# One core: four query projections and half of the output layer moved between the attention's steps, probabilities scaled on ScalarE

## The chip, the cores and the metric

The kernel runs on one core of a Trainium2 chip. The metric is the device time of one execution in microseconds (us). The engines are called by their short names: PE (TensorE, matrix multiply; PEld is its weight load), DVE (VectorE), ACT (ScalarE), POOL (GpSimd) and SP (SyncE, which issues the weight DMAs). They run their own instruction streams in order and wait for one another on semaphores.

## What is computed

One inference step of a two-layer decoder on T = 288 tokens: 256 of a prompt and 8 x 4 of eight samples. Layer 0 is a convolution module and a dense SwiGLU. Then keys and values are projected, and layer 1 is a sliding-window attention with a sink and a mixture of 8 experts. The change lies in the attention of layer 1:

```python
hq = rms_norm(h, P['g_attn_norm'][j])
q = rms_norm((hq @ P['w_q'][j]).reshape(N, T, N_KV_HEADS, GROUP, HEAD_DIM), P['g_q_norm'][j])
...
s = jnp.einsum('bnqkgd,bnskd->bnkgqs', qb, kb).astype(jnp.float32) * (HEAD_DIM ** -0.5)
s = s + rel_bias_heads(rel_bias, dist)
s = jnp.where(valid[None, :, None, None], s, -jnp.inf)
...
m = jnp.maximum(jnp.max(s, axis=-1, keepdims=True), sink)
p = jnp.exp(s - m)
denom = jnp.sum(p, axis=-1, keepdims=True) + jnp.exp(sink - m)
return jnp.einsum(eq, (p / denom).astype(v.dtype), v)
...
h = h + o @ P['w_o'][j]
```

There are 16 query heads of 64 channels in 4 groups, one key head for each group, and blocks of 128 positions; a query block sees itself and the block before.

## The kernel before

**Precision and weights.** Large products are made from three matmuls in fp32r (`mm3`, L352): high part by high part, high by low, low by high. Each weight unit of 128 x 2048 comes by DMA into one of six `land` buffers, ACT casts it into `w_hi` (`hi_to`), and DVE subtracts to make `w_lo` (`lo_to`), in a ring of four. PE frees a slot with `used`.

**Query projection** (L530 to L547). Eight tiles of 128 channels (two heads of two groups each), each 24 matmuls of 288 columns. ACT copies a tile to `Q`, POOL multiplies it by the token's inverse norm, ACT squares it, PE takes the mean over a head (`head_mean`), ACT takes the root, DVE makes the reciprocal and multiplies (`head_norm`, L1364).

**Attention** (L549 to L642). Nine steps in the order of `STEPS`: (n, b) is head group n with query block b (b = 0 has one key block, b = 1 two), and `None` is all samples. In a step PE makes the scores (`scores`), DVE adds the bias and finds the maximum (`soft_args`), ACT takes the exponentials (`exps`), DVE multiplies by the inverse sum (`normalise`, L1427), PE transposes the probabilities (`turn_probs`), ACT copies them out of PSUM (`pT`), and PE multiplies by the values (`attend`). After the second group of a pair ACT and DVE split the result into `H_hi` and `H_lo` (`o_hi`, `o_lo`).

**The order of the work** is written out by hand, on each engine for itself. At step s, PE issues scores(s+2), attend(s-1), turn_probs(s); DVE issues soft_args(s+1), normalise(s), o_lo(s-1); ACT issues exps(s+1), o_hi(s-1), and the pT copies of s. Between two steps PE has no other work, except five matmuls on constants ahead of the first transposes (`FILL`, L588).

**Output layer** (L674 to L687). Eight tiles of 24 matmuls with `w_o`; after each, the sums of two tiles earlier for the router (`route_sums`, `to_tokens`). Then the routing, the gathering of rows and the loop over experts, which is two thirds of the time.

## Time and profile before

| what | value |
|---|---|
| median of 3 runs | 1561.8 us (1558.99 to 1562.72) |
| the profiled execution | 1560.62 us |
| its span | 1558.8 us |
| mean granted TensorE clock | 0.986 of full speed |
| PE busy | 1520.7 us, 98% of the span, 7891 instructions |
| DVE, ACT, POOL busy | 1218.9, 969.2, 116.4 us |
| chain that ended last | PE 92%, DVE 3%, DMA 2%, ACT 1% |

The profiled execution is one run; its time is the span and some 2 us around it. Busy PE time is modelled at the ends of matmuls, which are pipelined, so that two matmuls that overlap both count. A granted clock of 1.00 is 2.4 GHz and 0.50 is 1.2 GHz. Times in a view count from the start of the span. An idle time in brackets stands before the instruction, with the one that released it.

### The profile page before, as it was taken

To read this page: it belongs to the slowest core of one execution; us is meant where nothing else is said; L and a number is where in the kernel's file an instruction comes from. 1 tells how busy PE (TensorE), PEld (TensorE's weight loads), DVE (VectorE), ACT (ScalarE), POOL (GpSimd) and SP (SyncE) were. 2 spreads that over 40 slices of the span, in tenths; PEclk is the share of its full clock that TensorE was granted. 3 is DMA by queue.
4 is the path that set the end of the run, shared out by engine and by line. 5 is a ranking of instruction groups with operands and counts; after the bars stand their busy time and mean duration, and the time that the engine had idled before them with its cause. 6 is when DMAs were issued, how large, how long until landed. Compare 5 with 4: busy or idle time off the path is not lost.

```text
span 1558.8 us, 22061 instructions
## 1 busy us (share of the span) xinstructions
PE 1520.7 (98%) x7891; PEld 1284.1 (82%) x7891; DVE 1218.9 (78%) x1237; ACT 969.2 (62%) x1072; POOL 116.4 (7%) x99
## 2 busy tenths in 40 slices
PE   8998999999989989999999999999999999999998
PEld 6986999999975968888888888888888888888776
DVE  6995545446696458888888889889889889889886
ACT  6554443344564247677777677777777677767764
POOL 1001011011320010000000000000000000000000
PEclk9999999999998979999999999999999999999999
DMA  8930345444531549989989998998998998998992
GB/s 348 175 128 27 108 162 177 144 156 150 187 123 50 193 177 372 367 310 404 398 321 385 395 356 349 401 381 321 412 373 314 422 370 309 423 377 300 414 366 106
DMA packets 66259, 438.48 MB, mean 281 GB/s; under 512 B 8069, under 2 KB 10373, under 8 KB 15648
## 3 DMA queue, kind: packets, MB, share of 16 engines
q1 hardware_dynamic: 57312, 412.38, 67.6%
q0 software_dynamic: 5552, 19.36, 5.1%
q10 hardware_dynamic: 3344, 6.05, 1.1%
q8 instruction: 33, 0.54, 0.1%
q14 instruction: 18, 0.15, 0.0%
HBM read 423.73 MB, written 15.03 MB: 281 GB/s over the span
## 4 chain that ended last, share of the span: by engine, by line
PE 92%; DVE 3%; DMA 2%; ACT 1%; issue 1%; POOL 1%; SPq 0%; ACTq 0%; DVEq 0%; POOLq 0%
PE bank L354 27%; PE bank L356 27%; PE bank L355 27%; PE bank L402 3%; PE bank L779 2%; DMA land<-in_w_expert 1%; PE bank L376 1%; DMA land<-in_w_dense 1%; PE bank L628 0%; PE bank L711 0%; PE bank L602 0%; PE bank L657 0%; PE bank L717 0%; PE bank L580 0%; PE bank L617 0%
## 5 line engine op out<-in xcount | busy, mean ns | idle before, releaser
L1474 DVE TENSOR_TENSOR w_lo<-land,w_hi 128x2048 fp32r<-128x2048 f32 x224 | 504.3, 2289 | 78.2 <-ACT w_hi L1078 76.3
L1078 ACT CAST w_hi<-land 128x2048 fp32r<-128x2048 f32 x224 | 418.5, 1913 | 6.4 <-issue 3.5
L354 PE MATMUL bank<-w_hi,xe_hi 128*128 128x512 f32 x896 | 364.8, 407 | 1.6 <-DVE xe_lo L1560 1.0
L356 PE MATMUL bank<-w_hi,xe_lo 128*128 128x512 f32 x896 | 354.3, 395 | 0.0
L355 PE MATMUL bank<-w_lo,xe_hi 128*128 128x512 f32 x896 | 353.0, 394 | 0.0
L1573 DVE TENSOR_TENSOR d_lo<-land,d_hi 128x2048 fp32r<-128x2048 f32 x112 | 256.8, 2292 | 44.6 <-ACT d_hi L1081 43.7
L1081 ACT CAST d_hi<-land 128x2048 fp32r<-128x2048 f32 x112 | 213.9, 1911 | 122.3 <-PE bank L356 119.1
L356 PEld LDWEIGHTS bank<-w_hi,xe_lo 128*128 128x128 f32 x896 | 168.4, 188 | 39.4
L354 PEld LDWEIGHTS bank<-w_hi,xe_hi 128*128 128x128 f32 x896 | 169.0, 189 | 36.2 <-DVE xe_lo L1560 1.2
L355 PEld LDWEIGHTS bank<-w_lo,xe_hi 128*128 128x128 f32 x896 | 169.1, 189 | 34.1
L354 PE MATMUL bank<-d_hi,heT_hi 128*128 128x512 f32 x448 | 177.3, 396 | 1.1 <-DVE heT_lo L1605 1.1
L355 PE MATMUL bank<-d_lo,heT_hi 128*128 128x512 f32 x448 | 177.1, 395 | 0.0
L356 PE MATMUL bank<-d_hi,heT_lo 128*128 128x512 f32 x448 | 176.3, 394 | 0.0
L1196 DVE TENSOR_TENSOR w_lo<-land,w_hi 128x2048 fp32r<-128x2048 f32 (+1 forms) x56 | 128.2, 2295 | 26.5 <-ACT w_hi L845 26.3
L354 PE MATMUL bank<-G_hi,w_hi 128*128 128x288 f32 x416 | 124.7, 300 | 0.3 <-PE bank L356 0.3
L355 PE MATMUL bank<-G_lo,w_hi 128*128 128x288 f32 x416 | 122.7, 295 | 0.0
L356 PE MATMUL bank<-G_hi,w_lo 128*128 128x288 f32 x416 | 122.3, 294 | 0.0
L845 ACT CAST w_hi<-land 128x2048 fp32r<-128x2048 f32 (+1 forms) x56 | 104.4, 1871 | 24.5 <-PE bank L356 22.2
L1153 ACT CAST heT_hi<-bank 128x256 fp32r<-128x256 f32 x112 | 41.8, 373 | 123.2 <-PE bank L779 123.2
L354 PEld LDWEIGHTS bank<-d_hi,heT_hi 128*128 128x128 f32 x448 | 84.2, 188 | 22.3 <-issue 2.5
L356 PEld LDWEIGHTS bank<-d_hi,heT_lo 128*128 128x128 f32 x448 | 84.5, 189 | 20.1
L355 PEld LDWEIGHTS bank<-d_lo,heT_hi 128*128 128x128 f32 x448 | 84.5, 189 | 19.0
(264 smaller groups left out, 2088.4 us busy)
## 6 DMA issues: line engine op xcount, KB each, us to landing
land<-in_w_expert SPq DMA_DIRECT2D x336, 1024.0 KB, 6.4
land<-in_w_dense SPq DMA_DIRECT2D x54, 1024.0 KB, 4.9
rel_rows<-rb POOLq DMA_DIRECT2D x1, 3072.0 KB, 36.1
bias<-rel_rows ACTq DMA_DIRECT2D x4, 512.0 KB, 4.8
y_rows<-zero_rows POOLq DMA_DIRECT2D x3, 512.0 KB, 10.8
X<-in_x SPq DMA_DIRECT2D x4, 288.0 KB, 5.7
out_y<-X SPq DMA_DIRECT2D x2, 576.0 KB, 2.8
Us<-in_state POOLq DMA_DIRECT2D x1, 1088.0 KB, 9.5
```

What stands on the lines that cost most here:

```text
L354: pe.matmul(out, w[0], x[0], start=start, stop=False)
L355: pe.matmul(out, w[0], x[1], start=False, stop=False)
L356: return pe.matmul(out, w[1], x[0], start=False, stop=stop)
L402: last = pe.matmul(bank[4 + m % 2][:, 0:SEQ], diag[:, g, w - taps[0], :], Up[:, PE_CHANNELS[m], w:w + SEQ], start=(w == 0), stop=(w == CW ...
L779: last = pe.transpose(bank[6][:, P * k:P * k + P], he[:, P * k:P * k + P], ident)
L845: act.copy(w_hi[n % RING][:, 0:cols], land[n % LAND][:, 0:cols]).then_inc(hi_done, 1)
L1078: act.copy(w_hi[n % RING][:], land[(DENSE + u) % LAND][:]).then_inc(hi_done, 1)
L1081: act.copy(d_hi[ch % 2][:], land[(DENSE + u) % LAND][:]).then_inc(d_hi_done, 1)
L1153: act.copy(heT_hi[:], bank[6][:, 0:CH]).then_inc(heT_hi_ready, 1)
L1196: dve.tensor_tensor(w_lo[n % RING][:, 0:cols], land[n % LAND][:, 0:cols], w_hi[n % RING][:, 0:cols].bitcast(F32), ALU.subtract).then_inc(s ...
L1474: dve.tensor_tensor(w_lo[n % RING][:], land[slot][:], w_hi[n % RING][:].bitcast(F32), ALU.subtract).then_inc(split, 1)
L1573: dve.tensor_tensor(d_lo[ch % 2][:], land[slot][:], d_hi[ch % 2][:].bitcast(F32), ALU.subtract).then_inc(d_split, 1)
```

## The change

- **Query tiles 4 to 7** leave the projection. Tiles 4, 5 and 6 stand behind scores(1), and tile 7 stands in step 1 of the attention.
- **The norm of the queries** is no longer applied to them. `Q` is the raw product times the gain; the mean squares are taken into narrow columns (`query_means`), ACT takes their roots (`query_root`), DVE the reciprocals (`query_scales`), and `soft_args` multiplies the scores by them, one instruction for each head (SCALAR_TENSOR_TENSOR) in place of one for each bank. For the samples POOL multiplies by `q_scale_s`. The roots of the second four tiles are taken by ACT in step 2.
- **The probabilities** are multiplied by ACT: DVE's `normalise` ends at the reciprocal, and ACT's new `normalise(s)` has four instructions and stands behind exps(s+1).
- **The output layer** is split by its input channels. `output_half` takes the first four (12 matmuls a tile) for tiles 0 to 4 in the steps behind the samples' and tiles 5 to 7 behind the last; DVE adds each to `X` (`add_half`). The other four stand where the layer was, 12 matmuls a tile.
- The samples' step moves from place 4 to 5; H and G change places, which lets the first bias DMAs go earlier; `FILL` goes; some `hi_to` and `lo_to` move into the steps.

The diff, cut to its core:

```diff
+            def query_means(t):
+
+                ng, g = divmod(t, GR)
+                out, at = MEANS[ng]
+                pe.wait_ge(kq_sq, 2 + t + 1)
+                if t == 0:
+                    pe.wait_ge(rt_ready, 1)
+                for b in range(2):
+                    pe.matmul(out[:, at + 2 * GR * b + 2 * g:at + 2 * GR * b + 2 * g + 2], sq[:, t % 2, P * b:P * b + P],
+                              c("mean_head")[:, 0:P:HD], start=True, stop=True)
+                a = at + 4 * GR + NS * g
+                pe.matmul(out[:, a:a + NS], c("mean_head"), sq[:, t % 2, SEQ:T], start=True, stop=True).then_inc(q_ms, 1)
...
-                if s == 4:
-                    pe.wait_ge(kq_ready, 2 + KT_D)
+                if STEPS[s] == (2, 1):
+                    pe.wait_ge(q_root, 4)
+                    pe.wait_ge(qs_sum, 2)
...
                 if s == 0:
-                    pe.wait_ge(kq_sd, 2 + KT_D)
-                    for _ in range(FILL):
-
-                        pe.matmul(bank[4][:, 0:256], ident, con[:, 0:256], start=True, stop=True)
+                    pe.wait_ge(kq_sd, 2)
                 pe.wait_ge(pn_ready, s + 1)
                 for m in range(TURNS[s], TURNS[s + 1]):
                     kb = m - TURNS[s]
+                    if m == 1:
+                        pe.wait_ge(kq_copied, 2 + 6)
...
+            pe.wait_ge(kq_copied, 2 + GR)
+            pe.wait_ge(kq_ready, 2)
             scores(0)
             scores(1)
+            query(4, bank[1])
+            pe.wait_ge(kq_sd, 2)
+            query(5, bank[5])
+            pe.wait_ge(kq_copied, 2 + 5)
+            query_means(4)
+            query(6, bank[1])
             for s in range(len(STEPS)):
-                if s + 2 < len(STEPS):
+                if s == 2:
+                    attend(1)
+                    pe.wait_ge(kq_copied, 2 + KT_D)
+                    query_means(7)
+                if s + 2 < len(STEPS) and s + 2 != SAMPLES:
                     scores(s + 2)
-                if s >= 1:
+                if s >= 1 and s != 2:
                     attend(s - 1)
+                if s > SAMPLES + 1:
+                    output_half(2 * (s - SAMPLES) - 3)
                 turn_probs(s)
+                if s > SAMPLES:
+                    output_half(2 * (s - SAMPLES) - 2)
+                if s == 1:
+                    pe.wait_ge(kq_copied, 2 + 7)
+                    query_means(5)
+                    query_means(6)
+                    query(7, bank[1])
+                if s + 2 == SAMPLES:
+                    scores(SAMPLES)
             attend(len(STEPS) - 1)
+            for d in range(5, KT_D):
+                output_half(d)
...
                 if d >= 4:
                     pe.wait_ge(x_attn, d - 3)
-                for k in range(KT_D):
-                    last = mm3(bank[d % 4][:, 0:T], wblock(n, KT_D * (d % 2) + k), H(k), k == 0, k == KT_D - 1)
+                elif d >= 2:
+                    pe.wait_ge(x_half, KT_D if d == 2 else KT_D - 1)
+                else:
+                    pe.wait_ge(s_ready, len(STEPS))
+                for k in range(GR, KT_D):
+                    last = mm3(bank[d % 4][:, 0:T], wblock(n, KT_D * (d % 2) + k), H(k), k == GR, k == KT_D - 1)
```

```diff
+            def query_copy(t):
+
+                act.wait_ge(kq_done, 2 + t + 1)
+                if t < 2:
+                    act.wait_ge(kq_ms, t + 1)
+                else:
+                    act.wait_ge(q_ms, t - 1)
+                src = bank[[0, 1, 2, 3, 1, 5, 1, 1][t]][:, 0:T]
+                act.activation(sq[:, t % 2, :], src, ACT.Square).then_inc(kq_sq, 1)
+                act.activation(Q[:, t, :], src, ACT.Identity, scale=g_q8[:, 0:1]).then_inc(kq_copied, 1)
+
+            def query_root(ng):
+
+                out, at = MEANS[ng]
+                act.wait_ge(q_ms, GR * ng + GR)
+                for b in range(2):
+                    a = at + 2 * GR * b
+                    act.activation(q_scale[:, b, ng, :], out[:, a:a + 2 * GR], ACT.Sqrt,
+                                   bias=eps_tok[:, b:b + 1]).then_inc(q_root, 1)
...
+            def normalise(s):
+
+                act.wait_ge(inv_ready, s + 1)
+                for g in range(GR):
+                    part = SS[:, g, :] if STEPS[s] is None else probs(s)[:, g, :]
+                    last = act.activation(part, part, ACT.Copy, scale=small[:, s % 2, 20 + g:21 + g])
+                last.then_inc(pn_ready, 1)
...
-            hi_to(DENSE)
+            hi_to(U_O + 2)
             exps(0)
+            query_copy(4)
             for s in range(len(STEPS)):
                 if s + 1 < len(STEPS):
                     exps(s + 1)
+                normalise(s)
+                if s == 0:
+                    query_copy(5)
+                    query_copy(6)
                 if s - 1 in OUT_STEPS:
                     o_hi(s - 1)
...
-                    act.wait_ge(kq_ready, 2 + KT_D)
+                    act.wait_ge(kq_ready, 2)
...
+                if s == 1:
+                    query_copy(7)
+                if s == 2:
+                    query_root(1)
+                    act.wait_ge(qs_sum, 2)
+                    act.activation(q_scale_s[:], q_scale_s[:], ACT.Sqrt).then_inc(qs_root, 1)
+                if s == 3:
+                    hi_to(U_O + 3)
+                if s == 5:
+                    hi_to(DENSE)
```

```diff
+            def query_scales(ng):
+
+                out, at = MEANS[ng]
+                dve.wait_ge(q_root, 2 * ng + 2)
+                seq(dve.reciprocal(q_scale[:, :, ng, :], q_scale[:, :, ng, :]))
+                a = at + 4 * GR
+                dve.tensor_tensor(q_scale_s[:, GR * ng:GR * ng + GR, :],
+                                  out[:, a:a + GR * NS].rearrange("p (g t) -> p g t", g=GR),
+                                  eps_col[:].unsqueeze(1).to_broadcast([P, GR, NS]), ALU.add).then_inc(qs_sum, 1)
+
+            query_scales(0)
...
+                ng, i = divmod(n, 2)
+                for g in range(GR):
+                    h, a = divmod(g * w, 512)
+                    last = dve.scalar_tensor_tensor(out=probs(s)[:, g, :], in0=bank[2 * (s % 2) + h][:, a:a + w],
+                                                    scalar=q_scale[:, b, ng, 2 * g + i:2 * g + i + 1],
+                                                    in1=bias[:, n % 2, g, 2 * P - w:2 * P], op0=ALU.mult, op1=ALU.add)
...
-                seq(dve.reciprocal(sm[:, 20:24], sm[:, 20:24]))
-                for g in range(GR):
-                    if STEPS[s] is None:
-                        part = SS[:, g, :]
-                    else:
-                        part = probs(s)[:, g, :]
-                    last = dve.tensor_scalar(part, part, sm[:, 20 + g:21 + g], None, ALU.mult)
-                last.then_inc(pn_ready, 1)
+                dve.reciprocal(sm[:, 20:24], sm[:, 20:24]).then_inc(inv_ready, 1)
...
             soft_args(0)
             for s in range(len(STEPS)):
                 if s + 1 < len(STEPS):
                     soft_args(s + 1)
+                if s == 0:
+                    lo_to(U_O + 2)
+                if s == SAMPLES + 2:
+                    add_half(0)
+                if s == SAMPLES + 3:
+                    add_half(1)
+                    add_half(2)
                 normalise(s)
-                if s == 0:
-
-                    head_norm(2 + KT_D - 1, Q[:, KT_D - 1, :], g_q8[:])
+                if s == 2:
+                    query_scales(1)
+                if s == 3:
+                    dve.wait_ge(qs_root, 1)
+                    dve.reciprocal(q_scale_s[:], q_scale_s[:]).then_inc(qs_ready, 1)
+                if s == SAMPLES:
+                    lo_to(U_O + 3)
                 if s - 1 in OUT_STEPS:
                     o_lo(s - 1)
+            add_half(3)
+            lo_to(DENSE)
+            add_half(4)
             o_lo(len(STEPS) - 1)
-            lo_to(DENSE)
+            for d in range(5, KT_D):
+                add_half(d)
```

Where it moves instructions. The first place is ACT's stream from the bias DMA behind the exponentials of step 1 to the four small DMAs ahead of those of step 2 (S is a probability buffer, Q the queries, bank the PSUM). Before:

```order
L1025 DMA bias<-rel_rows 128x4x256 [waits s_ready]
L1054 COPY pT<-bank 128x512 [waits pT_done]
L1065 DMA raw<-rel_rows 64x1x128 [waits kq_ready]
L1065 DMA small<-rel_rows 64x1x4
L1065 DMA raw<-rel_rows 64x1x128
L1065 DMA small<-rel_rows 64x1x4
```

After:

```order
L1110 DMA bias<-rel_rows 128x4x256 [waits s_ready]
L1117 ACTIVATE S<-S,small 128x128 [waits inv_ready]
L1117 ACTIVATE S<-S,small 128x128 x3
L1072 ACTIVATE sq<-bank 128x288 [waits q_ms,kq_done]
L1073 ACTIVATE Q<-bank,g_q 128x288
L1072 ACTIVATE sq<-bank 128x288 [waits q_ms,kq_done]
L1073 ACTIVATE Q<-bank,g_q 128x288
L1152 COPY pT<-bank 128x512 [waits pT_done]
L1163 DMA raw<-rel_rows 64x1x128 [waits kq_ready]
L1163 DMA small<-rel_rows 64x1x4
L1163 DMA raw<-rel_rows 64x1x128
L1163 DMA small<-rel_rows 64x1x4
```

The four scalings of step 0 and the copies of tiles 5 and 6 now stand ahead of the pT copy and the four small DMAs.

The second place is ACT's stream behind the pT copy of step 2, through the next exponentials, to the pT copies of step 3 (SS and S are probability buffers). Before:

```order
L1018 ACTIVATE SS,small<-SS,small 128x160 [waits nm_ready]
L1018 ACTIVATE SS,small<-SS,small 128x160 x3
L1020 ACTIVATE small<-small 128x4 [waits es_arg]
L1038 CAST H_hi<-bank 128x4x128 [waits pv_done]
L1054 COPY pT<-bank 128x512 [waits pv_done,pT_done] x2
```

After:

```order
L1081 ACT_TABLE_LOAD
L1081 ACTIVATE q_scale<-bank,eps_tok 128x8 [waits q_ms]
L1081 ACTIVATE q_scale<-bank,eps_tok 128x8
L1171 ACTIVATE q_scale_s<-q_scale_s 128x256 [waits qs_sum]
L1103 ACT_TABLE_LOAD
L1103 ACTIVATE S,small<-S,small 128x128 [waits nm_ready]
L1103 ACTIVATE S,small<-S,small 128x128 x3
L1105 ACTIVATE small<-small 128x4 [waits es_arg]
L1117 ACTIVATE S<-S,small 128x256 [waits inv_ready]
L1117 ACTIVATE S<-S,small 128x256 x3
L1131 CAST H_hi<-bank 128x4x128 [waits pv_done]
L1152 COPY pT<-bank 128x512 [waits pv_done,pT_done] x2
```

Two table loads, the roots of the second four tiles, and the scaling of step 3 now stand ahead of step 3's pT copies.

The third place is PE's stream around the transposes of steps 0 and 1. Before:

```order
L590 MATMUL bank<-con 128x256 [waits kq_sd]
L590 MATMUL bank<-con 128x256 x4
L602 MATMUL bank<-con,S 128x128 [waits pn_ready]
L602 MATMUL bank<-con,S 128x128 x3
L580 MATMUL bank<-K,Q 128x256 [waits s_ready]
L580 MATMUL bank<-K,Q 128x256 x3
L628 MATMUL bank<-pT,V 64x512 [waits pT_ready]
L602 MATMUL bank<-con,S 128x128 [waits pn_ready]
L602 MATMUL bank<-con,S 128x128 x3
L602 MATMUL bank<-con,S 128x128 [waits pT_ready]
L602 MATMUL bank<-con,S 128x128 x3
```

After:

```order
L603 MATMUL bank<-K,Q 128x128 [waits s_ready]
L603 MATMUL bank<-K,Q 128x128 x3
L627 MATMUL bank<-con,S 128x128 [waits pn_ready,kq_sd]
L627 MATMUL bank<-con,S 128x128 x3
L606 MATMUL bank<-K,Q 128x256 [waits s_ready]
L606 MATMUL bank<-K,Q 128x256 x3
L656 MATMUL bank<-pT,V 64x512 [waits pT_ready,qs_sum,q_root]
L627 MATMUL bank<-con,S 128x128 [waits kq_copied,pn_ready]
L627 MATMUL bank<-con,S 128x128 x3
L627 MATMUL bank<-con,S 128x128 [waits pT_ready]
L627 MATMUL bank<-con,S 128x128 x3
```

The fill is gone, the third scores stand ahead of the first transposes as before, and the three query tiles ahead of them (not shown) are what PE now does while the first softmax runs.

## Rows read from the trace of the kernel before

**Rows 1.** Busy time by stage: us, busy (instructions) of PE, PEld, DVE, ACT, POOL, PEclk, DMA.

```profile
446.00:507.00 61.00, 54.14 (x262) 36.01 (x263) 43.17 (x122) 34.70 (x110) 5.22 (x10) 0.83 0.28 93
507.00:549.00 42.00, 40.94 (x311) 39.40 (x310) 19.12 (x30) 11.96 (x17) 2.65 (x5) 0.96 0.48 179
...
580.00:1550.00 970.00, 967.56 (x4325) 782.03 (x4323) 844.51 (x638) 690.40 (x574) 44.80 (x17) 1.00 0.91 359
```

**Rows 2.** PE in order of time: start, us, line, instruction, count, [idle before, releaser].

```profile
415.45 0.40 PE L354 MATMUL bank<-G_hi,w_hi 128*128 128x288 f32 x1
...
434.32 0.51 PE L354 MATMUL bank<-G_hi,w_hi 128*128 128x288 f32 x1
...
437.59 0.29 PE L356 MATMUL bank<-G_hi,w_lo 128*128 128x288 f32 x1
...
447.72 0.75 PE L508 MATMUL bank<-sq,con 128*128 128x288 f32 x2 [0.92 <-ACT sq L969]
...
453.24 4.07 PE L590 MATMUL bank<-con 128*128 128x256 f32 x10
...
463.27 1.87 PE L602 MATMUL bank<-con,S 128*128 128x128 f32 x8 [2.24 <-DVE S L1438]
...
471.70 0.66 PE L602 MATMUL bank<-con,P 128*128 128x128 f32 x4
...
482.21 2.11 PE L617 MATMUL bank<-sq,VC 128*128 128x32 f32 x16
...
485.40 3.62 PE L617 MATMUL bank<-sq,VC 128*128 128x32 f32 x16
...
503.10 1.93 PE L628 MATMUL bank<-pT,V 128*64 128x512 f32 x4 [0.24 <-ACT pT L1054]
506.43 0.40 PE L354 MATMUL bank<-H_hi,w_hi 128*128 128x288 f32 x1 [1.40 <-DVE H_lo L1453]
```

**Rows 3.** Granted TensorE clock (the number behind PE busy) in stretches of 2 us.

```profile
484.00:486.00 2.00, 2.00 (x7) 0.50 0.00 0
...
498.00:500.00 2.00, 1.96 (x8) 1.00 0.00 0
```

**Rows 4.** ACT in order of time, steps 0 to 2.

```profile
452.61 1.28 ACT L1018 ACT_TABLE_LOAD   x1
453.91 0.40 ACT L1018 ACTIVATE S<-S,small 128x128 f32<-128x128 f32 x1
...
456.17 0.51 ACT L1018 ACTIVATE S<-S,small 128x256 f32<-128x256 f32 x1 [0.52 <-DVE small L1423]
...
458.25 0.56 ACT L1054 COPY pT<-bank 128x512 f32<-128x512 f32 x1
459.85 0.63 ACTq L1065 DMA_DIRECT2D raw<-rel_rows  x1
...
462.45 0.40 ACT L1018 ACTIVATE P<-P,small 128x128 f32<-128x128 f32 x1 [3.64 <-DVE small L1423]
```

**Rows 5.** DVE in order of time, steps 0 and 1.

```profile
451.41 0.69 DVE L1415 TENSOR_TENSOR S<-bank,bias 128x512 f32<-128x512 f32 x1 [1.53 <-DMA bias<-rel_rows]
...
453.20 1.28 DVE L1415 TENSOR_TENSOR S<-bank,bias 128x512 f32<-128x512 f32 x2
454.52 1.22 DVE L1420 TENSOR_REDUCE small<-S 128x4 f32<-128x1024 f32 x1
...
461.93 1.29 DVE L1438 TENSOR_SCALAR S<-S,small 128x256 f32<-128x256 f32 x4
```

**Rows 6.** ACT, eight of the diagonals in a row (L879).

```profile
105.60 2.44 ACT L879 ACTIVATE diag<-con,w_dw 128x128 f32<-128x128 f32 x8 [2.95 <-PE bank L402]
```

**Rows 7.** DVE, two taps of the convolution in a row (L1252).

```profile
100.13 0.48 DVE L1252 SCALAR_TENSOR_TENSOR C<-Up,w_dw,C 128x256 f32<-128x256 f32 x1
100.53 0.48 DVE L1252 SCALAR_TENSOR_TENSOR odd<-Up,w_dw,odd 128x256 f32<-128x256 f32 x1
```

**Rows 8.** The bias DMA on the page: issues, KB each, us from issue to landing.

```profile
bias<-rel_rows ACTq DMA_DIRECT2D x4, 512.0 KB, 4.8
```

131 lines of the change are left out of this document (78 added, 53 removed).

## The prediction, made before the changed kernel was run

> **What bounds the kernel now.** I read the table by stage first. In the loop over experts (the stretch from 580 to 1550 us) PE is busy without a gap at full clock [rows 1]: what starts this loop earlier or later shifts the end by as much, one for one. The change lies ahead of it, between the first query tile at 415.45 us and the first output matmul at 506.4 [rows 2]. The attention's stretch (446 to 507) is where something is to be had: its granted clock is 0.83, and no engine is busy throughout (PE 54 of 61 us, DVE 43, ACT 35) [rows 1]. Next comes PE's timeline with its idle times [rows 2]: PE waits for the squares (0.92), for the first softmax (it does the fill for 4.07), for the scaled probabilities of step 1 (2.24), and 1.40 for the last H_lo. Then the clock [rows 3]: from 484 to some 497 us it is at 0.50 of full, the 1.2 GHz level, after a stretch in which PE did matmuls of 32 columns, and the same 16 small matmuls that took 2.11 us take 3.62 [rows 2].
>
> **What the change moves.** A query tile of 24 matmuls takes 3.27 us (434.32 to the last start at 437.59, 0.133 us a matmul, with the last one [rows 2]). Four of them leave the projection, some 12.8 us, and half of the output layer leaves its place, 96 matmuls at the same 0.133 us, 12.8 us. PE's own work stays what it was. The narrow head means need three small matmuls in place of one wide one; I take 0.65 us for both (0.75 for the wide one [rows 2]). So the gain can only be waits of PE that the 25.6 us fill. What can be filled is at most the 14.0 us of waits and fill that I count below, 1.5 us ahead of them, and the loss by the half clock.
>
> **How I count.** I laid the streams of the engines out one beside another, each instruction starting when its engine and what it waits for are through, with durations from the rows, at full clock: four transposes 0.55 (0.66 with their tail), the product with the values for two key blocks 1.93 [rows 2]. For the kernel before, from its first scores on, this gives the transposes of step 1 at 463.4 (the trace has 463.27) and the first output matmul at 503.3 (the trace has 506.43 [rows 2]). I put the 3.1 us between down to the half clock. The sum of PE's waits in the layout, fill included, is 14.0 us, and 1.5 between the last query tile and the first scores.
>
> **Prices on ACT and DVE.** An exponential of 128 elements takes a slot of 0.40 us, of 256 elements 0.51, with a small one of 0.2 behind four [rows 4], so exps is 1.8 (one key block) or 2.2 (two). A scaling on ACT is not in the trace. The nearest row is the diagonals' multiply by a column, 128x128: eight in 2.44 us [rows 6], 0.29 from start to start with 0.1 left at the end. At 256 elements I add 0.11, the difference of the two exponentials [rows 4]. Four are then 1.27 or 1.70 us. Bounds: 0.9 and 1.35 if the column costs nothing, 1.6 and 2.0 if it costs what an exponential does. On DVE four of 256 cost 1.29 [rows 5]. DVE's scale-and-add for 256 elements is 0.48, and 0.40 from start to start [rows 7], so four are 1.67 where two wide adds were 1.28, and 1.13 for 0.69 with one block [rows 5]. Bounds: no dearer than the adds, or 0.48 each. With the maximum of 1.22 [rows 5] and some 0.3 of small instructions soft_args is 3.2. DVE is relieved of eight wide reciprocals, but seven of these lie beside PE's query matmuls now and give nothing; the eighth lies beside the wait of step 1.
>
> **The decisive point is the order on ACT.** Before, the scaling of step s follows soft_args(s+1) on DVE, and runs beside ACT's exps(s+1). Now it stands behind exps(s+1), on the same engine. PE's transposes of step s therefore wait for soft_args(s+1), exps(s+1) and the scaling in a row: 3.2, 2.2 and 1.7 us with two key blocks. In the layout of the changed kernel (the clock of the trace before, first query tile again at 415.5, rounded) it comes out so:
>
> - Scores 0 and 1 run at 431 to 434, the bias, issued at 430.5, lands at 435.2 or a little later (4.8 us by the page [rows 8]; today DVE waits 1.53 for it [rows 5]), and tiles 4 to 6 keep PE at work until 444.2. Step 0's probabilities are scaled by 444.8. This part works as meant: the fill and 1.5 us of waits go.
> - Then ACT copies tiles 5 and 6 (1.5 us), pT (0.5) and issues four small DMAs, which hold it from 459.85 to 462.45, 2.5 us [rows 4]; exps(2) 1.8 and the scaling of step 1, 1.7, end at 452.8. PE is through at 448.7: **4.1 us of wait**, where there were 2.2.
> - Step 2: tile 7's copy, exps(3), scaling: PE waits 1.1 and 0.7.
> - Step 3: behind pT(2), at 464.4, ACT loads the table of the root (1.28 [rows 4]), takes the roots (0.5 and, behind a DVE step, 0.3), and loads the exponential's table again. DVE's soft_args(4) stands behind query_scales(1), which waits for the roots, so its maximum is ready only at 468.9. exps(4) 1.8 and the scaling 1.7 end at 472.4. PE has nothing to do from 465.4: **7.1 us**.
> - Step 4: soft_args of the samples waits for scores(5), which PE ends at 478.0; exps and scaling follow: 2.4 us.
> - Step 5: o_hi(3) stands behind the scaling of step 4, o_lo(3) behind it, soft_args(6), exps(6) and the scaling of step 5 behind these, to 492.3; PE is free from 486.8: **5.6 us**.
> - Behind the samples the halves of the output layer fill well: 1.4, 1.8 and 0.2 us of wait are left, and the three tiles at the end hide o_lo(8), which cost 1.40.
>
> Sum of the waits: 4.1 + 1.1 + 0.7 + 7.1 + 2.4 + 5.6 + 1.4 + 1.8 + 0.2 = 24.4 us, against 15.5 before: 8.9 more, less small gains in the means, 8.3. The second halves start at 524.4; with 12.8 us of the layer done, this stands for 511.6 against 503.3 at full clock and against 506.4 in the trace. In the output layer and its routing sums PE is busy 40.94 of 42 us, DVE 19.12 and ACT 11.96 [rows 1]; with 12.8 us of PE's work gone, the 29 left still cover both, so nothing is late there.
>
> **The clock** comes on top. Before it cost 3.1 us. Now there are more and longer pauses ahead of PE's work (4.1, 7.1, 5.6), and the samples' small matmuls, ahead of which it stood at 0.50, still come, right behind the longest of them. If as much work as before, or twice as much, is done at 1.2 GHz, the price is 3 to 6 us; if the moved matmuls keep the clock up, 0. I take 3, as before. The sum is then 8.3 us over the profiled execution's 1560.6 (span 1558.8 and 1.8 around it): 1568.9, and with the 1.2 us by which the median of 1561.8 stands above that execution, **1570**.
>
> By the Trainium skill (ScalarE: Activation LUTs, "What ACT_TABLE_LOAD costs") a switch of table sets is 1.28 us and some 1.4 of drain besides, 2.66 in all, and one should group the functions by set; this change takes a root amid exponentials, with two switches. The row [rows 4] shows the load of 1.28 at 452.61 and the first exponential at 453.91, with no drain between, so I count 1.28. By the page's figure the two switches would cost 2.7 us more, and the estimate would be 2 us higher.
>
> **Rivals.**
> - *The gaps fill as meant.* PE's 14 us of waits and the half clock are taken up by the 25.6 us, since ACT's chain is shorter than I count and keeps ahead. For it: ACT was busy only 35 of 61 us in this stretch [rows 1], and the steps behind the samples do fill in the layout. Against it: ACT's own work in the stretch grows by 13 us of scaling, 3.4 of tile copies and 2.6 of tables, to some 55 of 90 us, and the wait at a step is for its chain, not for its share. It decides if soft_args, exps and scaling in a row come under PE's work in a step (some 6 to 8 us). It gives 6 to 14 us less: 1553.
> - *A draw.* The lower bounds hold: scaling at 0.9 and 1.35 (2.6 us less in the layout), the scale-and-add no dearer than the add (1.6 less), and no loss by the clock (3.1 less). 8.3 - 7.3 = 1.0: 1563.
> - *The clock falls for long.* From the 7.1 us pause on through the samples' step PE stands at 1.2 GHz; scores(8), both parts of attend(5) and the transposes, 8 us of work, take twice as long. 1570 + 6: 1576.
> - *ACT's waits are less serial.* That the four DMA issues don't hold ACT, or lie in a wait, takes 1.6 us; it alone changes no sign.
>
> **Chances and range.** Forecast as worked out 0.50, the draw 0.22, the long half clock 0.15, the filled gaps 0.13. What one can tell from no change here is some 0.3%, 4.7 us. Below 1557.1 lies the filled case, 0.13; between 1557.1 and 1566.5 the draw and the forecast's lower edge, 0.25; above, 0.62. The range is 1559 to 1577: from the draw's lower side to the long half clock. The forecast's own range is 1565 to 1575.
>
> **What would show it.** Right: between the transposes of step 2 and those of step 3 PE idles for 6 us or more, released by ACT; two table loads of 1.28 stand there; PE waits some 4 us ahead of step 1's and some 5 ahead of step 5's transposes; the released-by engine of the transposes is ACT everywhere; the stretch from the first query tile to the end of the routing sums is longer than the 133 us of now; the loop over experts is unchanged. Wrong: scaling slots below 0.3 us, waits ahead of the transposes under 2 us, a clock of 1.00 through the stage, or a changed loop over experts.

## The result, and the profile after

The changed kernel takes **1578.6 us** (median of 4 runs, 1577.2 to 1580.0) against 1561.0 us in the same session (4 runs): a ratio of 1.0113, 95% interval 1.0096 to 1.0131, so 17.6 us slower. Forecast were 1570 and at most 1577. The profiled execution has a span of 1575.4 us, 16.6 more than before. Two executions of all those below (1742 us of the kernel before, 3017 us of h1) fell far out of line, and every median and ratio here is of the others.

By stage (columns as in [rows 1]; the first stretch starts at the first query tile, which [rows 2] have at 415.45):

```profile
417.00:450.00 33.00, 32.24 (x234) 30.54 (x234) 16.85 (x33) 21.52 (x49) 0.81 (x1) 1.00 0.39 131
450.00:540.00 90.00, 72.51 (x377) 55.74 (x376) 36.12 (x100) 42.91 (x126) 4.88 (x10) 0.77 0.21 69
...
597.00:1567.00 970.00, 967.34 (x4325) 782.28 (x4323) 844.67 (x639) 691.09 (x575) 44.78 (x17) 1.00 0.91 359
```

The loop over experts is what it was in [rows 1]: 4325 matmuls and 967.3 us of PE in 970. The loss lies ahead of it. The last routing sum (L661 before, L726 after) starts here:

```profile
548.00 0.64 PE L661 MATMUL bank<-pick,con 128*128 128x32 f32 x2
```
```profile
565.00 0.64 PE L726 MATMUL bank<-pick,con 128*128 128x32 f32 x2
```

That is 17.0 us later. The first query matmul is 1.9 us later already (417.33 against 415.45); the section on why the prediction was right or wrong says where that arises.

PE's timeline, after. It answers to [rows 2]: look at what stands in brackets, and at the samples' products (128x32), 3.62 us both, where [rows 2] have 2.11 and 3.62.

```profile
455.42 1.09 PE L627 MATMUL bank<-con,S 128*128 128x128 f32 x8 [3.12 <-ACT S L1117]
...
477.45 1.97 PE L627 MATMUL bank<-con,S 128*128 128x128 f32 x8 [6.81 <-ACT S L1117]
...
490.22 0.66 PE L627 MATMUL bank<-con,S 128*128 128x128 f32 x4 [2.02 <-ACT S L1117]
...
498.12 1.97 PE L625 MATMUL bank<-con,SS 128*128 128x128 f32 x8 [3.71 <-ACT SS L1117]
...
504.87 3.62 PE L642 MATMUL bank<-sq,VC 128*128 128x32 f32 x16
...
509.57 3.62 PE L642 MATMUL bank<-sq,VC 128*128 128x32 f32 x16
```

L1117 is ACT's new scaling. It ends the waits ahead of steps 1, 3, 4 and 5, as forecast, and the waits are no longer than forecast: 3.1, 6.8, 2.0 and 3.7 us for 4.1, 7.1, 2.4 and 5.6. What is much longer than forecast is the time at 1.2 GHz. PE's busy time and, behind it, the granted clock, in stretches chosen at its turns (here the columns are PE, PEclk, DMA):

```profile
456.00:464.00 8.00, 8.00 (x41) 0.57 0.01 2
464.00:474.00 10.00, 5.63 (x25) 1.00 0.18 52
474.00:481.00 7.00, 3.55 (x20) 0.51 0.23 46
481.00:491.00 10.00, 7.98 (x71) 1.00 0.62 215
491.00:519.00 28.00, 23.61 (x83) 0.51 0.11 38
519.00:535.00 16.00, 16.00 (x95) 1.00 0.20 65
```

Three falls, each in or behind a pause of PE: the one of 3.1 us, the one of 6.8, the one of 2.0. The third lasts some 27 us; the stretch of 28 us shown for it holds 23.6 us of PE's work. Before, the long fall was 13 us ([rows 3] show its first part and that it was over at 498):

```profile
484.00:497.00 13.00, 13.00 (x41) 0.50 0.00 0
```

ACT around step 3, after; it answers to [rows 4]. The roots stand behind pT, between two table loads, and the scaling behind exps(4):

```profile
469.53 1.28 ACT L1081 ACT_TABLE_LOAD   x1
470.83 0.43 ACT L1081 ACTIVATE q_scale<-bank,eps_tok 128x8 f32<-128x8 f32 x2
471.90 0.42 ACT L1171 ACTIVATE q_scale_s<-q_scale_s 128x256 f32<-128x256 f32 x1 [0.65 <-DVE q_scale_s L1503]
472.33 1.28 ACT L1103 ACT_TABLE_LOAD   x1
474.06 0.40 ACT L1103 ACTIVATE S<-S,small 128x128 f32<-128x128 f32 x1 [0.44 <-DVE small L1549]
...
475.70 1.69 ACT L1117 ACTIVATE S<-S,small 128x256 f32<-128x256 f32 x4
```

DVE beside it; it answers to [rows 5]. It waited 16.3 us for the roots, and only then could scale and add the scores of step 4:

```profile
471.29 0.25 DVE L1501 RECIPROCAL q_scale<-q_scale 128x16 f32<-128x16 f32 x1 [16.26 <-ACT q_scale L1081]
...
471.78 1.12 DVE L1541 SCALAR_TENSOR_TENSOR S<-bank,q_scale,bias 128x128 f32<-128x128 f32 x4
```

### The profile page after: what moved, and what is told of

Read it like the earlier page. It is cut to its first block, busy times and chain, and to the rows that moved or that the text cites. A ratio compares the mean times of both kernels' runs of the same rounds, so it can differ in the third digit from the quotient of the medians.

```text
span 1575.4 us, 22112 instructions
## 1 busy us (share of the span) xinstructions
PE 1529.0 (97%) x7913; PEld 1293.5 (82%) x7913; DVE 1197.6 (76%) x1221; ACT 981.9 (62%) x1107; POOL 106.7 (7%) x91
## 4 chain that ended last, share of the span: by engine, by line
PE 92%; DVE 3%; ACT 2%; DMA 1%; issue 1%; POOL 0%; ACTq 0%; DVEq 0%; SPq 0%; POOLq 0%
PE bank L363 27%; PE bank L365 27%; PE bank L364 27%; PE bank L411 3%; PE bank L847 2%; DMA land<-in_w_expert 1%; PE bank L385 1%; PE bank L627 0%; PE bank L642 0%; PE bank L779 0%; PE bank L785 0%; PE bank L722 0%; PE bank L606 0%; PE bank L718 0%; PE bank L656 0%
## 5 line engine op out<-in xcount | busy, mean ns | idle before, releaser
L1714 DVE TENSOR_TENSOR d_lo<-land,d_hi 128x2048 fp32r<-128x2048 f32 x112 | 256.7, 2292 | 43.9 <-ACT d_hi L1189 42.9
L363 PE MATMUL bank<-G_hi,w_hi 128*128 128x288 f32 x368 | 109.2, 297 | 0.3 <-PE bank L365 0.3
L365 PE MATMUL bank<-G_hi,w_lo 128*128 128x288 f32 x368 | 109.5, 298 | 0.0
L364 PE MATMUL bank<-G_lo,w_hi 128*128 128x288 f32 x368 | 109.4, 297 | 0.0
L363 PE MATMUL bank<-H_hi,w_hi 128*128 128x288 f32 x320 | 101.4, 317 | 7.7 <-POOL H_lo L1792 4.4
```

Source lines behind the costliest of these rows:

```text
L363: pe.matmul(out, w[0], x[0], start=start, stop=False)
L364: pe.matmul(out, w[0], x[1], start=False, stop=False)
L365: return pe.matmul(out, w[1], x[0], start=False, stop=stop)
L1714: dve.tensor_tensor(d_lo[ch % 2][:], land[slot][:], d_hi[ch % 2][:].bitcast(F32), ALU.subtract).then_inc(d_split, 1)
```

## The layout, with the clock put in

The layout of the prediction can be run again with two things of the trace put in: the first query tile at 417.1, 1.6 us later than the 415.5 of the prediction (the trace has 417.33), and PE's work at half speed in the stretches 456.5 to 462.6, 475 to 480.8 and 491.2 to 518.9 (by the granted clock the falls run from 457.1 to 463.9, 474.2 to 481.0 and 491.2 to 518.5). It then ends the routing sums at 565.3 us; the trace has 565.4, counted as 0.4 us behind the start of the row of L726 above. An agreement of 0.1 us is closer than such inputs allow. At full clock the layout ends them at 551.8. So the half clock cost **13.5 us**, where I had put 3. For the kernel before the layout ends them at 541.9 and the trace at 548.4: 6.5. The 17.0 us are then 8.3 of waits (the forecast's own figure, as the layout is the same), 1.6 of later start (1.9 between the two first matmuls), and 13.5 - 6.5 = 7.0 of clock, together 16.9.

The traces give a split of their own, without the layout. From the first query matmul to the end of the last routing sum, in stretches of 1 us, PE is idle or busy, and of its busy time the share (1 - granted clock) is lost to the clock:

| kernel | PE idle | lost to the clock | PE's work at full clock | length |
|---|---|---|---|---|
| before | 9.0 | 11.8 | 112.2 | 133.2 |
| changed | 19.2 | 17.8 | 111.0 | 148.3 |
| e2 (scaling on VectorE) | 14.4 | 13.1 | 111.5 | 139.3 |
| e3 (before, scaling on ACT) | 14.0 | 21.6 | 111.4 | 147.1 |
| e4 (scaling ahead of the exponentials) | 13.8 | 11.3 | 111.6 | 136.7 |

The changed kernel has 10.2 us more idle time, 6.0 more lost to the clock and 1.2 less work, since the five fillers are gone: 15.0 of the 15.1 by which the stretch is longer. The late start makes it 17.0. Two methods thus give 8 to 9 us of waits and 6 to 7 of clock. (Some work at half clock lies where PE would have waited anyway, so the column is no price by itself.)

The experiments test this sum: the ACT part by undoing it, doing it alone and reordering it, the clock part by fillers. Theory A is the sum. The main rivals: the interleaving itself costs the time; ACT's busy time costs it, wherever it stands; the clock makes no difference.

## The experiments

Ratios are to the kernel before, run on the same chip in the same session (its medians: 1561.1, 1560.6, 1560.2 and 1561.5).

**e1_fill.** PE kept at work in its waits.

```diff
+FILL = {1: 4, 3: 12, 4: 3, 5: 8}
...
+                if s in FILL:      # in turn_probs, once the bank is free
...
+                    for _ in range(FILL[s]):
+                        pe.matmul(bank[4 + m % 2][:, 0:256], ident, con[:, 0:256], start=True, stop=True)
                 pe.wait_ge(pn_ready, s + 1)
```

> The changed kernel with PE kept at work in its waits: 4, 12, 3 and 8 matmuls of 128x256 on the identity ahead of the transposes of steps 1, 3, 4 and 5 (0.43 us each at 2.4 GHz, 0.85 at 1.2 GHz, so 11.6 us at full clock, all inside waits of 3.1, 6.8, 2.0 and 3.7 us or close to them). Theory A, the half clock is what made the loss larger than forecast: my layout with the measured half-clock stretches put in ends the routing sums at 565.3 us (the trace has 565.4) and without them at 551.8, so the granted clock is 0.95 or more from 450 to 535 us, the two samples' products take 2.1 instead of 3.6 us each, and the time falls by some 10 to 13 us, to 1565-1569. Rival B, PE's clock is incidental since ACT's and DVE's chain sets the pace: the time stays within 3 us of 1578.6 though the clock is up. Rival C, these fillers don't hold the clock up: clock as in the changed kernel, time 1578-1590, since the fillers then take twice their length.

Measured: 1571.9 us, 1.0063 [1.0040, 1.0087], so 6.8 us less than the changed kernel with 27 matmuls more. PEclk, first e1, then the changed kernel in the same stretches:

```profile
476.00:504.00 28.00, 24.53 (x158) 18.20 (x157) 15.83 (x43) 18.64 (x52) 4.12 (x8) 1.00 0.39 126
504.00:520.00 16.00, 15.32 (x74) 12.15 (x74) 5.42 (x16) 8.41 (x31) 0.00 (x0) 0.68 0.01 2
```
```profile
476.00:504.00 28.00, 20.82 (x115) 14.61 (x116) 12.37 (x35) 16.81 (x48) 4.12 (x8) 0.68 0.39 126
504.00:520.00 16.00, 15.32 (x59) 12.55 (x60) 5.04 (x15) 5.04 (x17) 0.00 (x0) 0.55 0.00 1
```

The clock stays up from 476 to 504. PE does nothing more of use there, and the time falls: B and C are out. But A's range of 1565 to 1569 is missed, and the gain is some half of what it gave. One reason is that the clock falls again at 506, in the middle of the samples' product, with PE busy throughout:

```profile
503.64 1.97 PE L651 MATMUL bank<-sq,VC 128*128 128x32 f32 x16
...
506.17 3.11 PE L651 MATMUL bank<-sq,VC 128*128 128x32 f32 x16
```

Another lies ahead of every filler. This trace has a fall between 435 and 442 us, with PE busy, that the changed kernel's trace doesn't have (PEclk 1.00 there):

```profile
435.00:442.00 7.00, 7.00 (x27) 0.51 0.57 217
```

From the first query matmul to the transposes of step 0 it takes 34.5 us here and 31.4 there, so this fall cost 3.1 us. The traces of h1 and h3 have it too. A third, behind the wait ahead of step 1, came in spite of the four fillers there.

**e2_scale_on_dve.** One part undone.

```diff
-                normalise(s)     # on ACT
...
-                dve.reciprocal(sm[:, 20:24], sm[:, 20:24]).then_inc(inv_ready, 1)
+                seq(dve.reciprocal(sm[:, 20:24], sm[:, 20:24]))
+                for g in range(GR):
+                    last = dve.tensor_scalar(part, part, sm[:, 20 + g:21 + g], None, ALU.mult)
```

> The changed kernel with one part undone: the probabilities are scaled on VectorE again (four multiplies behind the reciprocal), ACT has no scaling. The moved query tiles and output halves stay. Theory A (the transposes wait for soft_args, exps and the scaling in a row, because the scaling stands behind the next exps on ACT): by the layout at full clock the waits ahead of steps 1, 3, 4 and 5 fall from 4.1, 7.1, 2.4, 5.6 us to 0.6, 5.2, 0.5, 3.9 and the end comes 9.7 us earlier: 1569, and down to 1560 if the shorter waits also shorten the stretch at 1.2 GHz. Rival B (the loss comes from the interleaving itself, such as the roots and table loads in step 3 and the small matmuls behind it, and ACT's scaling is free): 1575-1580.

Measured: 1570.7 us, 1.0069 [1.0046, 1.0092], 7.9 us less than the changed kernel; the rival is out, the gain is a little below A's smallest. The waits are as laid out (5.0, 0.4 and 3.4 us at steps 3, 4 and 5):

```profile
468.84 1.97 PE L626 MATMUL bank<-con,S 128*128 128x128 f32 x8 [4.97 <-DVE S L1554]
...
483.22 0.66 PE L626 MATMUL bank<-con,S 128*128 128x128 f32 x4 [0.43 <-DVE S L1554]
...
489.39 1.09 PE L624 MATMUL bank<-con,SS 128*128 128x128 f32 x8 [3.42 <-DVE SS L1554]
```

The routing sums end at 555.8, the layout at full clock says 542.1: the half clock costs 13.7 us, no less than in the changed kernel. That shorter pauses would shorten it was wrong. And e2 is still 9.6 us slower than the kernel before: the moved work, with the roots amid the exponentials, gains nothing by itself. By the traces e2 has 5.4 us more idle time than the kernel before. What is left of the 9.6 wasn't taken apart by leaving out the query tiles, or the output halves, alone.

**e3_before_scale_on_act.** One part alone, in the kernel before.

```diff
-                seq(dve.reciprocal(sm[:, 20:24], sm[:, 20:24]))
-                (and the four multiplies)
+                dve.reciprocal(sm[:, 20:24], sm[:, 20:24]).then_inc(inv_ready, 1)
+                normalise(s)     # on ACT, behind exps(s + 1)
```

> The kernel before with one part of the change alone: ACT scales the probabilities, behind the next step's exps. Query projection and output layer as before. Theory A: by the layout the waits ahead of the transposes grow (steps 0, 1, 3, 4, 6: 2.9, 3.8, 2.2, 1.3, 4.3 us) and the time by 10.5 us at full clock: 1571, more (to 1578) if longer waits lengthen the half clock. Rival B (ACT has room, busy 35 of 61 us): 1559-1563, no change.

Measured: 1574.5 us, 1.0086 [1.0065, 1.0106], 13.3 us slower than the kernel before. The one part makes a loss as large as three quarters of the change's, without any work moved:

```profile
467.89 1.97 PE L603 MATMUL bank<-con,S 128*128 128x128 f32 x8 [3.13 <-ACT S L1033]
...
480.92 1.64 PE L603 MATMUL bank<-con,S 128*128 128x128 f32 x8 [2.00 <-ACT S L1033]
```

The two losses don't add: 9.6 (e2) and 13.3 (e3) together are 22.9, the whole change costs 17.6. By the table above two thirds of e3's loss are clock: 5.0 us more idle, 9.8 more lost to the clock.

**e4_scale_ahead_of_exps.** The changed kernel, same instructions in another order.

```diff
+                normalise(s)               # ACT
                 if s + 1 < len(STEPS):
                     exps(s + 1)
-                normalise(s)
+                normalise(s)               # VectorE: sum and reciprocal
                 if s + 1 < len(STEPS):
                     soft_args(s + 1)
```

> The changed kernel with the same instructions on the same engines in another order: ACT scales step s ahead of exps(s+1), and VectorE forms the sum and reciprocal of step s ahead of soft_args(s+1). Theory A (the order on ACT is the cost, not the price of a scaling on ACT): by the layout the end comes 8.5 us earlier at full clock (wait ahead of step 5's transposes 1.1 instead of 5.6, of step 3's 4.6 instead of 7.1): 1570, down to 1562 with less half clock. Rival B (it is ACT's busy time that costs): 1577-1580. Rival D (VectorE now stands still until exps(s) is through, which makes a new chain): 1580 or more.

Measured: 1567.0 us, 1.0043 [1.0028, 1.0059], 11.6 less than the changed kernel. Both rivals are out: it is the order, since ACT and VectorE do the same work. The edit changes both engines' order together, so how much is ACT's alone isn't shown. Ahead of step 5 PE waits 0.81 us instead of 3.71:

```profile
469.13 1.97 PE L627 MATMUL bank<-con,S 128*128 128x128 f32 x8 [3.32 <-ACT S L1117]
...
487.12 1.09 PE L625 MATMUL bank<-con,SS 128*128 128x128 f32 x8 [0.81 <-ACT SS L1117]
```

**i1_before_act_ahead.** The same order in the kernel before (edit as e3's with e4's order).

> The kernel before with the scaling on ACT (as e3), but ordered as in e4: ACT scales step s ahead of exps(s+1), VectorE forms the sum and reciprocal ahead of soft_args(s+1). Theory A (place in the order and busy time on ACT both count; here nothing of the projection or output layer fills PE's waits): by the layout at full clock the end lies 3.8 us ahead of e3's and 6.7 behind the kernel before's: 1567-1571. Rival (only the order counts, so this is as good as VectorE's scaling): 1559-1563. Rival (without the moved work the order is worth nothing): 1573-1576, as e3.

Measured: 1568.7 us, 1.0052 [1.0034, 1.0070]: 5.8 us less than e3, still 7.2 slower than the kernel before, as A has it. So ACT's scaling costs something even in the better order. That this is for want of work in PE's waits is argued, not shown.

**g4_roots_early.** No roots amid the exponentials.

The kernel leaves out the second half's own means, so it computes something else, and only its time is of use.

```diff
+                for half in range(2):      # both halves from the first group's means
+                    ... act.activation(q_scale[:, b, half, :], ..., ACT.Sqrt, ...)
-                if s == 2:
-                    query_root(1)
-                    ...
```

> The changed kernel without the second group of roots amid the exponentials: heads 8 to 15 are scaled by the means of heads 0 to 7, taken with the first group (this changes the computation: the second half's own root mean squares are left out of the scaling), so two table loads of 1.28 us, the roots, and the wait of VectorE for them go from step 3. Theory A: the wait of PE ahead of step 3's transposes falls from 6.8 us to some 3, the end at full clock comes 2.6 us earlier (the other waits grow a little), and the half clock that follows this pause at 475 us may not come: 1568-1576. Rival (the 6.8 us wait moves on to step 4 or 5 and the clock falls as before): 1577-1580.

Measured: 1575.0 us, 1.0096 [1.0077, 1.0114], 3.6 less than the changed kernel, within A's range. The wait ahead of step 3 falls from 6.81 to 3.12 us, and the third fall of the clock comes all the same:

```profile
486.00:514.00 28.00, 23.34 (x86) 0.52 0.10 38
```

So of the longest wait only half was the table loads and roots, and the longest wait was not what made the clock's long stretch.

**g1_reordered.** e4, and further links of the chain loosened.

```diff
+                if s == 1:                 # PE: ahead of turn_probs(1), was behind it
+                    query_means(5); query_means(6); query(7, bank[1])
+                if s == 1: query_copy(7)   # ACT: ahead of pT's copies, was behind them
+                if s == 2: query_root(1)   # with the samples' roots, likewise
-            act.dma_start(dst[...])        # the samples' four small DMAs
+            pool.dma_start(dst[...])
```

> e4 (scaling ahead of the next exps) with the rest of the serial chain loosened: the last query tile stands ahead of the transposes of step 1 instead of behind them, its copy and the second roots on ACT stand ahead of pT's copies, and the samples' four small DMAs go out from POOL's queue instead of holding ACT 2.6 us. Theory A (order on ACT): layout at full clock ends 12.3 us ahead of the changed kernel's and 3.8 ahead of e4's (waits left: about 4 us ahead of step 3, 2 for the samples' scaled queries, 1 ahead of step 5, 2 ahead of the samples' product): 1563, if the half clock costs the 10.4 us that it cost in e4. Rival (these pieces lie in waits anyway and the next link of the chain takes their place): 1566-1569, no better than e4.

Measured: 1562.3 us (10 runs), 1.0014 [1.0003, 1.0025]. That is 16.4 us less than the changed kernel, with the scaling still on ACT, and 4.8 less than e4; A's number is met.

**g2_reordered_fill.** g1 with fillers in waits and ahead of the samples' products.

```diff
+FILL = {3: 8, 5: 2}
+                        for _ in range(4):  # ahead of each of the samples' products
+                            pe.matmul(out, ident, con[:, 0:256], start=True, stop=True)
```

> g1 with fillers on PE: 8 matmuls of 128x256 ahead of the transposes of step 3, 2 ahead of step 5's, and 4 ahead of each of the two products of the samples (8 there; 18 in all, 7.7 us at 2.4 GHz, of which some 5 us lie in waits and 3 on the path). Theory A (the clock is what is left over of the difference, and it can be held up by wide matmuls where narrow ones or waits let it fall): granted clock near 1.0 to the end of the output layer, half-clock price 3 us or less instead of 10: 1563 - 7 + 3 = 1559, within 1556-1562. Rival (the clock falls all the same, fillers only add): 1564-1570.

Measured: 1566.9 us, 1.0038 [1.0024, 1.0053], 4.7 us slower than g1. A's expectation failed, but the test is a weak one. The clock falls before 494, and the first of the samples' products starts only at 495.19: the fall stands behind a wait of 1.99 us that no filler covers, since the fillers stand behind it. The eight on the path then run at 1.2 GHz in part:

```profile
491.53 2.58 PE L648 MATMUL bank<-con 128*128 128x256 f32 x8 [1.99 <-ACT stats L1173]
```

By the split of the traces g2 does 8.2 us more work than g1 and saves 1.6 of idle time and 1.3 of clock.

**g3_before_no_fill.** The kernel before without its five fillers.

```diff
-                    for _ in range(FILL):
-                        pe.matmul(bank[4][:, 0:256], ident, con[:, 0:256], start=True, stop=True)
```

> The kernel before without its five fillers ahead of step 0's transposes (the change takes them out as well). At full clock the layout gives the same end, since they lie in a wait. If they hold the clock up, the granted clock is lower between 452 and 470 and the time is 2 to 4 us longer: 1563-1565. If they only stand in the way of the transposes (they ran at half clock, 4.07 us, and delayed step 0): 1558-1561.

Measured: 1559.3 us (10 runs), 0.9997 [0.9986, 1.0008]: no difference that can be measured. The first fall is longer without them (PEclk 0.55 from 452 to 467, before 0.77), the second shorter (0.65 from 484 to 497, before 0.50), and the two about make up for each other, as the second of the two expectations has it:

```profile
452.00:467.00 15.00, 10.36 (x33) 0.55 0.39 123
484.00:497.00 13.00, 13.00 (x54) 0.65 0.00 0
```

**h2_dve_scale_fill, h3_samples_pt_first, h1_best_try.** e2 with fillers, 11, 4 and 8, in its three waits; g1 with the samples' pT copied ahead of exps(6) and the roots behind pT's copies again; and h3 with fillers, 10, 4 and 2, in its waits.

```diff
+FILL = {3: 10, 5: 2}                      # h1; h2: {3: 11, 5: 8}
+                    for _ in range(4):    # h1 and h2, ahead of the samples' scores
+                        pe.matmul(bank[2 * (s % 2)][:, 0:256], ident, con[:, 0:256], start=True, stop=True)
                     pe.wait_ge(qz_ready, 1)
-                if s + 1 < len(STEPS):    # h1 and h3, ACT
+                if s + 1 < len(STEPS) and s != SAMPLES:
                     exps(s + 1)
...
+                if s == SAMPLES:          # behind the samples' pT
+                    exps(s + 1)
```

> e2 (the changed kernel, probabilities scaled on VectorE as before, query tiles and output halves moved) with fillers in its waits: 11 matmuls of 128x256 ahead of step 3's transposes, 4 ahead of the samples' scores, 8 ahead of step 5's (9.9 us at 2.4 GHz, in waits of 5.0, 1.9 and 3.4 us). It says what moving the work between the attention's steps is worth by itself with the clock held up. By the layout e2 and the kernel before end alike at full clock (542.1 and 541.9); the half clock cost 13.5 us in e2 and 6.5 in the kernel before. Theory A: fillers bring e2's to 6 or less, 1562-1564. Rival C (clock falls behind the narrow matmuls anyway): 1567-1571, as e2.

> g1 with two places on ACT in another order: the second roots are behind pT's copies again (as in the changed kernel), and the samples' pT is copied ahead of exps(6), whose place cost PE a wait of 2.0 us in g1. Layout: end 0.7 us ahead of g1's. Theory A: 1559-1562, the 2.0 us wait gone, the 2.6 us wait for pT behind the roots gone and one of some 4 us ahead of step 3's transposes in its place. Rival: the half clock grows with the longer pause, 1563-1566.

> h3 (same call) with fillers only in waits: 10 matmuls of 128x256 ahead of the transposes of step 3, 4 ahead of the samples' scores, 2 ahead of step 5's transposes (6.9 us at 2.4 GHz, all in waits of 4.6, 1.8 and 1.1 us by the layout). Theory A (the half clock follows pauses of PE): the granted clock stays at 1.00 from 464 to 492, where g1 had 10 us at 0.50, and the time falls by 4 to 5 us against h3: 1556-1558, faster than the kernel before. Rival C (the half clock follows the narrow matmuls of the samples, whatever stands in the waits): it falls behind 480 all the same, and the time is within 2 us of h3.

Measured: h2 1564.3 us, 1.0024 [1.0008, 1.0040]; h3 1562.4 us, 1.0014 [1.0005, 1.0023]; h1 1561.3 us, 1.0005 [0.9994, 1.0015]. h2 is at A's upper end, 6.4 us less than e2, and by its interval still slower than the kernel before. First e2, then h2, from 440 to 492 and then to the end of the fall:

```profile
440.00:492.00 52.00, 39.77 (x250) 0.89 0.30 90
492.00:512.00 20.00, 19.32 (x66) 0.52 0.15 52
```
```profile
440.00:492.00 52.00, 49.10 (x311) 1.00 0.30 92
492.00:504.00 12.00, 11.32 (x58) 0.72 0.20 83
```

h3 came slightly above A's range. h1 did not do what A gave (1556 to 1558): it is 1.1 us below h3, within the 2 us of rival C, though its clock was higher from 464 to 492 (0.94 against 0.82). One fall is left between 464 and 472 (0.79), another comes during the samples' product. No version was found that beats the kernel before; h1 and g3 can't be told from it.

The layout against the traces, for the end of the routing sums. The layouts of the kernels with fillers leave these out. So the last column also holds fillers on the path; the start of each trace (the first query matmul at 416.4 in g3, 416.7 in e1 and e2, 416.9 in e3 and i1, 417.7 in g1, 417.9 in g2 and h2), while the layouts of g3, e3 and i1 start at the 415.5 of the kernel before and the others at 417.1; and in e1, h1 and h3 the fall between 435 and 442, worth some 3 us.

| kernel | layout, full clock | trace | difference |
|---|---|---|---|
| before | 541.9 | 548.4 | 6.5 |
| changed | 551.8 | 565.4 | 13.6 |
| e1 (fillers) | 551.8 | 561.7 | 9.9 |
| e2 (scaling on VectorE) | 542.1 | 555.8 | 13.7 |
| h2 (e2 with fillers) | 542.1 | 549.0 | 6.9 |
| e3 | 552.4 | 563.7 | 11.3 |
| i1 | 548.6 | 557.0 | 8.4 |
| e4 | 543.3 | 553.7 | 10.4 |
| g1 | 539.5 | 550.3 | 10.8 |
| h3 | 538.8 | 552.4 | 13.6 |
| h1 (h3 with fillers) | 538.8 | 550.1 | 11.3 |
| g2 (g1 with fillers) | 539.5 | 555.6 | 16.1 |
| g4 | 549.2 | 560.6 | 11.4 |
| g3 | 541.9 | 547.4 | 5.5 |

The layout orders waits well. The last column, 5.5 to 16 us and most of it the clock's, it does not give, and it differs by more than most edits are worth. Each kernel has one trace, and falls such as the one at 435 come in some traces and not in others of much the same code, so differences of 3 us in this column say little.

## Why the prediction was right or wrong

- **Direction and mechanism: right.** ACT's scaling, standing behind the next step's exponentials, ends the waits ahead of steps 1, 3, 4 and 5; undoing it gives back 7.9 us (e2), doing it alone costs 13.3 (e3), and moving it in the order, together with VectorE's part, gives back 11.6 (e4). It isn't the whole: without it e2 is still 9.6 us slower than the kernel before, which the layout at full clock puts level with it (542.1 and 541.9).
- **Prices: right.** Four scalings took 1.27 and 1.69 us (1.27 and 1.70 forecast), the scale-and-add 1.12 for one block (1.13), a table load 1.28. (The 3.27 us given for a query tile run to the start of its last matmul; the sums go by 96 times 0.133, so nothing hangs on it.)
- **The table loads.** By the Trainium skill (ScalarE: Activation LUTs, "What ACT_TABLE_LOAD costs") some 1.4 us of drain would come on top. In the rows of step 3 the root starts 0.02 us behind the end of its load (469.53 + 1.28 = 470.81, and 470.83): the trace has none there, nor ahead of the second load (471.90 + 0.42 = 472.32, and 472.33), and the row was the right source.
- **The waits: close, and rather too long in the forecast.** Step 5's was 3.7 instead of 5.6; PE's work ahead of it ran at 1.2 GHz in part, so that PE came to it later.
- **The step that failed: "I take 3, as before".** The clock term was mis-sized, and with 3 us put on both sides the sum of 8.3 had no change of the clock's cost in it at all. By the layout it measured 13.5 us, 7.0 more than before; by the split of the traces 6.0 more was lost. "Before cost 3.1" was read at the first output matmul; up to the end of the routing sums it was 6.5. The prediction had the facts for more: it named three pauses ahead of PE's work and put none of them into the price. The rival "the clock falls for long" described what happened, had 0.15, and was priced at 6 us for 8 us of work; the third fall held some 23 us of it. Its 1576 came nearest to the 1578.6, which lie above the stated range of 1559 to 1577.
- **Not foreseen: the later start of 1.9 us.** It has two parts. The first, 1.3 us, differs from trace to trace with no regard to the change. 0.8 us are there at 102 us (a row of the convolution starts at 102.78 against 101.94), and 0.4 come by a short half clock between 145 and 155 us; first the kernel before, then the changed one:

```profile
145.00:155.00 10.00, 6.60 (x44) 1.00 0.01 2
```
```profile
145.00:155.00 10.00, 6.57 (x34) 0.83 0.00 1
```

  Of the traces here only the one of the kernel before is without this fall; e3, whose code is the same as that up to 448 us, g3 and i1 have it too, and at 180 us e3 is 1.4 us late and g3 1.0. I take this part for a matter of the single execution, so part of the 16.6 us between the profiled spans isn't the change's; the medians (17.6) don't settle how much.

  The second part, 0.6 us, belongs to the change. From 180 us to the first query matmul every one of the ten kernels with the moved work loses 0.6 to 0.7 us, and e3, g3 and i1 lose none. In these two traces it arises in the dense layer, at full clock and with no idle time between the matmuls: from the first of the following rows to the second it takes 75.10 us before and 75.69 after. Why the same matmuls run 0.8% slower there stays open.

```profile
287.19 0.37 PE L354 MATMUL bank<-G_hi,w_hi 128*128 128x288 f32 x1 [0.30 <-PE bank L356]
...
362.29 0.37 PE L354 MATMUL bank<-A_hi,w_hi 128*128 128x288 f32 x1 [0.47 <-POOL A_lo L1672]
```
```profile
288.48 0.37 PE L363 MATMUL bank<-G_hi,w_hi 128*128 128x288 f32 x1 [0.30 <-PE bank L365]
...
364.17 0.38 PE L363 MATMUL bank<-A_hi,w_hi 128*128 128x288 f32 x1 [0.48 <-POOL A_lo L1813]
```
- **Open.** Whether the half clock accounts for all of the 13.5 us was shown only in part: fillers gave back 6.8 us in the changed kernel and 6.4 in e2, the rest rests on the layout's agreement with the trace (565.3 and 565.4) and on the split of the traces. What starts the fall during the samples' product, or the one at 435 us, wasn't settled.

## What to carry to other kernels

Before work is moved to an idle engine, look at what it will stand behind there: the same scalings, four in each step, cost 11.6 us more behind the next step's exponentials than ahead of them (5.8 in the kernel before: e3 and i1), though the engine was busy half the time (42.9 of 90 us). Filling PE's waits with real work moved from elsewhere pays only where the waits exist independently of the engines that feed it; here even e2, without ACT's scaling, had 14.4 us of idle time on PE where the kernel before had 9.0. And a forecast for a stage with pauses or narrow matmuls needs a term for PE's clock of its own, with the long case priced by all of PE's work up to the next stage.

## What the runs showed of the hardware

- The clock fell in two situations. In or behind a pause: 3.1, 6.8 and 2.0 us in the changed kernel. And with no pause: in e1, h1 and h3 near 435 us, and during the samples' product, whose 32 matmuls are 32 columns wide: in h2 PE is busy without a gap from 485.8 until the fall; the products run from 491.5 to 496.9, and PEclk is 1.00 up to 496 and 0.51 in the next 2 us:

```profile
492.08 1.97 PE L652 MATMUL bank<-sq,VC 128*128 128x32 f32 x16
...
494.60 2.33 PE L652 MATMUL bank<-sq,VC 128*128 128x32 f32 x16
```
```profile
494.00:496.00 2.00, 2.00 (x16) 1.00 0.48 201
496.00:498.00 2.00, 2.00 (x12) 0.51 0.00 0
```

- Useless matmuls in a pause can be worth more than they cost: 27 of them made the changed kernel 6.8 us faster, 23 made e2 6.4 us faster. With eight of 18 on the path (g2) they cost 4.7 us, and five taken out of the kernel before (g3) made no difference.
- How long the clock stayed down differed a lot. In the changed kernel it came back within 7 us twice, the first time under a full load (8.0 us of work in the 8 from 456 to 464, PEclk 0.57), and stayed down some 27 us the third time, with two more pauses but 23.6 us of PE's work in the 28 from 491 to 519. Before, it stayed down 13 us with PE busy throughout.
